# A two-layer hybrid decoder trunk on 8 cores: attention by parts of 512 keys in a ring, transposed by DMAs, with its statistics on GpSimd

## The chip, the cores and the metric

The kernel runs on 8 cores of one Trainium2 chip. Each core computes one of the 8 batch entries by itself; the cores exchange nothing. The metric is the device time in microseconds (us) of the slowest core. An execution is profiled on every core, and the profile shown is that of the slowest.

## The reference

Two layers, each with a sub-layer that mixes tokens in three parallel branches and one that mixes channels. B = 8, S = 2048, D = 1024; h @ w_in gives 7168 columns. Cut to what matters here:

```python
h = rmsnorm(x, norm_mix_pre[l]); z = h @ w_in[l]
za, zq, zk, zv, zc, zg = split(z)
ya = gmlp_branch(gelu(za), ...)                 # chunks of 128, 4 groups
yb = diff_attention(zq, zk, zv, lambda ...)     # 4 heads, q and k of 2 x 64, v of 128
yc = pool_branch(zc, w_pool, pool_scale)
merged = sum_i sigmoid(zg_i) * (y_i @ w_branch_i)
x = x + rmsnorm(merged @ w_out[l], norm_mix_post[l])
h = rmsnorm(x, norm_ffn_pre[l])
x = x + rmsnorm((silu(h @ Wg) * (h @ Wu)) @ w_ffn_out[l], norm_ffn_post[l])   # d_ff = 2816

# diff_attention, per block of 128 queries and head:
sc = q_c @ k_c.T * 64**-0.5                     # c = 0, 1; causal
w = softmax(sc_0) - lam * softmax(sc_1)
out = rmsnorm(w @ v, subln_g) * (1 - lambda_init)
```

## The kernel before, in words

Activations lie with features on the partitions. The work is cut into four stages (layer, half of the sequence): (0, 0), (0, 1), (1, 0), (1, 1), called stage 0 to 3. The feed-forward part of a stage's tokens runs in the next stage, beside that stage's attention; the last one's runs alone at the end. A stage is: projections K, V, Q; then, from stage 1 on, the feed-forward part of the stage before (`FG`, `FU` into `aT`, and `F` out of it); then the gMLP and pool branches (`gu`, `gv`, `pp` and small matmuls `mx`, `pm`, `pw`); gates of branches 0 and 2 (`G`, `B`, 16 pairs for each); gate of branch 1, which is attention's (`C` blocks); and the output projection (`O`). Behind `O` and `F` stands a norm, `tail`: sums over features by a matmul with ones (`SS`), ScalarE's `rs`, VectorE's `xn` (the residual added in `R7`), again squares and sums, and `h`, the next input in `HB`.

Attention goes by units: a unit is 128 queries and one head, 32 units in a stage. Before the change a unit's keys come in parts of up to 1024 (`key_chunks`). For each part TensorE makes both components' scores (`qk`, L1201; the diagonal's mask L1205), VectorE the row maximum (`max`, L1521), ScalarE the exponential (`exp`, L1346) into `PB`, which holds two units. Then VectorE makes the unit's factors from the sums (`w`, small operations L1422, L1551, L1425, and for two parts the rescaling L1543) and combines both components (`wk`, L1425). For every 512 keys TensorE transposes the combined weights by matmuls with the identity (`tr`, L1215), ScalarE copies the result to `WT` (`wt`), and TensorE multiplies it with V (`pv`, L1230). After four heads, ScalarE sums squares (`oc`), GpSimd makes the norm's factor (`f`), ScalarE scales (`y`), TensorE transposes (`yt`, L1241), and ScalarE writes `QY` (`ye`).

The order of each engine's work is written out beforehand by a planner, the class `Order`. It lets dense work pass one group at a time, and between groups puts in what its own clock calls ready: first `pv`, then `tr`, then the next `qk` when the progress of the dense work has reached that part's target. It has a duration for each operation, 0.2 us of lag between engines, and for a DMA its issue, its MB / 0.28, and 2.0 us. Every engine then runs its list in order and waits on semaphores. What attention has left at the fifth `C` group is run there without dense work (`finish_attention`). Weights come as blocks into four slots `WS`, cast by DMAs that GpSimd issues (`load`, L913); a block is loaded when TensorE has used the block four before. SP issues the loads of x (`x0`), of the residuals (`xo`, `xr` into `XR`, three places, each waiting for the `xn` three before), and the stores of x (`store`, 2 MB at once, when the last `xn` of a half is done).

## Time and profile before

| | |
|---|---|
| median of 3 runs | 2512.78 us (2510.51 to 2515.93) |
| profiled execution | 2516.2 us, span of its slowest core 2514.7 us |
| spans of the 8 cores | 2495.1 to 2514.7 us |
| mean granted TensorE clock, core 0 | 0.961 of 2.4 GHz |
| busy: TensorE, weight loads | 2289.6 us (91%), 1078.9 us |
| busy: VectorE, ScalarE, GpSimd | 1453.5 us (58%), 1275.8 us (51%), 289.4 us (12%) |
| mean DMA | 92 GB/s, HBM read 345 MB, written 34 MB |

Busy time is the time in which at least one instruction of the engine runs. Idle time is put down to what ended it. A group's line number is that of `kernel.py`; operations recorded by a helper have the helper's line (L1039 for dense matmuls, L1425, L1422 and L1283 for VectorE's and ScalarE's helpers), so there the tiles' names tell them apart: `ps<-HB,WS` is a matmul into PSUM from `HB` and `WS`. The timeline merges instructions of one kind that follow each other; its first two columns are the start and the length in us. The clock is the share of 2.4 GHz that the throttle granted.

### The profile page before, as it was taken

To read this page: it belongs to the slowest core of one execution; us is meant where nothing else is said; L and a number is where in the kernel's file an instruction comes from. 1 tells how busy PE (TensorE), PEld (TensorE's weight loads), DVE (VectorE), ACT (ScalarE), POOL (GpSimd) and SP (SyncE) were. 2 spreads that over 40 slices of the span, in tenths; PEclk is the share of its full clock that TensorE was granted. 3 is DMA by queue.
4 is the path that set the end of the run, shared out by engine and by line. 5 is a ranking of instruction groups with operands and counts; after the bars stand their busy time and mean duration, and the time that the engine had idled before them with its cause. 6 is when DMAs were issued, how large, how long until landed. Compare 5 with 4: busy or idle time off the path is not lost.

```text
span 2514.7 us, 39549 instructions; the slowest of 8 cores (2495.1 to 2514.7 us)
## 1 busy us (share of the span) xinstructions
PE 2289.6 (91%) x12332; PEld 1078.9 (43%) x12568; DVE 1453.5 (58%) x2618; ACT 1275.8 (51%) x2728; POOL 289.4 (12%) x573
## 2 busy tenths in 40 slices
PE   5999689999998997999998999999999899888996
PEld 2444344444443443444444444444444444333442
DVE  2467626777657884545524754567765778364313
ACT  2556635555675663634445542645667566442122
POOL 1111000000111100011011210001111111100011
PEclk9999789999998997999999999999999999889998
DMA  8433337333344442644346346643334533865458
GB/s 193 66 51 58 86 59 159 59 57 54 59 83 134 69 85 61 150 87 68 60 64 150 80 64 150 136 70 60 55 53 71 153 58 51 172 138 99 78 73 199
DMA packets 83369, 230.87 MB, mean 92 GB/s; under 512 B 8288, under 2 KB 9056, under 8 KB 82144
## 3 DMA queue, kind: packets, MB, share of 16 engines
q0 software_dynamic: 49456, 150.43, 38.0%
q1 hardware_dynamic: 33712, 77.91, 9.6%
q8 instruction: 108, 1.77, 0.3%
q14 instruction: 93, 0.76, 0.1%
HBM read 345.16 MB, written 33.55 MB: 151 GB/s over the span
## 4 chain that ended last, share of the span: by engine, by line
PE 81%; DMA 6%; DVE 5%; issue 4%; ACT 3%; POOL 0%; SPq 0%; another core or an unknown queue 0%; DVEq 0%; ACTq 0%; POOLq 0%
PE ps L1039 57%; PE ps L1080 11%; DMA WS<-wblk 4%; PE ps L1201 3%; PE ps L1130 2%; PE ps L1230 2%; PE ps L1215 2%; DVE st L1521 1%; DVE R L1425 1%; DMA R<-xT 1%; DVE R L1422 1%; PE ps L1205 1%; DVE TM L1425 1%; ACT WT L1283 1%; PE ps L1145 1%
## 5 line engine op out<-in xcount | busy, mean ns | idle before, releaser
L1039 PE MATMUL ps<-HB,WS 128*128 128x512 bf16 x4987 | 1165.7, 384 | 42.6 <-DMA WS<-wblk 19.8
L1039 PEld LDWEIGHTS ps<-HB,WS 128*128 128x128 bf16 x5120 | 493.2, 99 | 626.1 <-issue 88.7
L1283 ACT ACTIVATE TG<-ps 128x512 f32<-128x512 f32 x368 | 219.6, 597 | 526.2 <-PE ps L1039 518.7
L1521 DVE TENSOR_REDUCE st<-ps 128x1 f32<-128x1024 f32 (+7 forms) x384 | 343.2, 907 | 154.7 <-PE ps L1205 139.5
L1346 ACT ACTIVATE PB<-ps,st 128x1024 bf16<-128x1024 f32 (+7 forms) x384 | 331.2, 865 | 139.8 <-DVE st L1521 122.3
L1425 DVE SCALAR_TENSOR_TENSOR TM<-TG,ps 128x512 f32<-128x512 f32 x304 | 208.4, 686 | 321.1 <-PE ps L1039 169.9
L913 POOL DMA_DIRECT2D WS<-wblk x334 | 181.6, 544 | 1821.7 <-PE ps L1039 1472.0
L1080 PE MATMUL ps<-R,WS 128*128 128x512 bf16 x1371 | 313.2, 379 | 6.8 <-DMA WS<-wblk 2.9
L1283 ACT ACTIVATE R<-ps 128x512 f32<-128x512 f32 (+1 forms) x256 | 149.3, 596 | 230.9 <-PE ps L1080 108.9
L1039 PE MATMUL ps<-R,WS 128*128 128x512 bf16 x988 | 240.3, 381 | 6.6 <-DVE R L1422 1.9
L1425 DVE SCALAR_TENSOR_TENSOR PB<-PB,st 128x512 bf16<-128x512 bf16 (+3 forms) x320 | 204.4, 665 | 3.6
L1080 PEld LDWEIGHTS ps<-R,WS 128*128 128x128 bf16 x1408 | 133.7, 98 | 160.7 <-issue 13.4
L1039 PE MATMUL ps<-WS,HB 128*128 128x512 bf16 x747 | 184.2, 399 | 18.5 <-DMA WS<-wblk 14.2
L1283 ACT ACTIVATE WT<-ps 128x512 bf16<-128x512 f32 (+3 forms) x320 | 162.0, 532 | 72.5 <-PE ps L1215 71.4
L1283 ACT ACTIVATE HB<-R 128x512 bf16<-128x512 f32 x256 | 156.4, 628 | 38.4 <-DVE R L1422 18.2
L1039 PEld LDWEIGHTS ps<-R,WS 128*128 128x128 bf16 x1024 | 96.7, 98 | 115.0 <-issue 14.0
L1422 DVE TENSOR_TENSOR R<-TM,ps 128x512 bf16<-128x512 f32 x176 | 120.4, 684 | 40.1 <-PE ps L1039 36.6
L1230 PE MATMUL ps<-V,WT 128*128 128x128 bf16 x1088 | 110.1, 227 | 25.4 <-ACT WT L1283 23.3
L1215 PE MATMUL ps<-ident_s,PB 128*128 128x128 bf16 x1088 | 108.7, 225 | 22.4 <-DVE PB L1425 17.9
L1039 PEld LDWEIGHTS ps<-WS,HB 128*128 128x128 bf16 x768 | 75.7, 102 | 110.1 <-issue 37.4
L1230 PEld LDWEIGHTS ps<-V,WT 128*128 128x128 bf16 x1088 | 80.2, 101 | 74.8 <-issue 39.8
L1130 PE MATMUL ps<-HB,ones 128*128 128x512 bf16 x253 | 69.4, 421 | 46.9 <-ACT HB L1283 46.8
(90 smaller groups left out, 1708.9 us busy)
## 6 DMA issues: line engine op xcount, KB each, us to landing
WS<-wblk POOLq DMA_DIRECT2D x188, 512.0 KB, 5.5
WS<-wblk POOLq DMA_DIRECT2D x74, 352.0 KB, 4.6
xm<-R SPq DMA_DIRECT2D x8, 2048.0 KB, 9.5
XR<-xm SPq DMA_DIRECT2D x64, 256.0 KB, 6.3
WS<-wblk POOLq DMA_DIRECT2D x40, 384.0 KB, 5.6
R<-xT SPq DMA_DIRECT2D x16, 512.0 KB, 12.2
WS<-wblk POOLq DMA_DIRECT2D x32, 256.0 KB, 6.6
x<-R SPq DMA_DIRECT2D x4, 2048.0 KB, 10.7
```

Source lines behind the costliest of these rows:

```text
L913: e.dma_start(out=WS[:, m % NSLOT, 0:n], in_=src).then_inc(*inc(f"WS{m % NSLOT}", block, 16))
L1039: mm = e.matmul(bank(b), lh, rh, start=i == 0, stop=i == len(pairs) - 1)
L1080: mm = e.matmul(bank(C.bank[key]), w[:, k, :], aT[:, part * 11 + k, tile_of(t)], start=part == 0 and k == 0, stop=part == 1 and k == 10)
L1130: mm = e.matmul(bank(C.bank[key]), ones[:], h_buffer(kind, s)[:, c, tile_of(t)], start=c == 0, stop=c == 7)
L1201: mm = e.matmul(ps[:, 2 * comp + b, 0:m], QY[cs, h, qb * 128:(qb + 1) * 128], KT[cs, h, first + 512 * p:first + 512 * p + m], start=True, ...
L1215: mm = e.matmul(ps[:, C.bank[key], (k % 4) * 128:(k % 4 + 1) * 128], PB[:, u % 2, 0, k * 128:(k + 1) * 128], ident[:], start=True, stop=True)
L1230: mm = e.matmul(ps[:, O_BANK, h * 128:(h + 1) * 128], WT[:, rnd % 2, (k % 4) * 128:(k % 4 + 1) * 128], V[:, k, h * 128:(h + 1) * 128], sta ...
L1283: e.activation(out=out, in_=in_, func=func, scale=scale, bias=bias).then_inc(*inc(sem, key))
L1346: e.activation(out=PB[:, par, comp, first:first + n], in_=src, func=AF.Exp, bias=st[:, par, nm + comp:nm + comp + 1], scale=1.0, accum_out ...
L1422: e.tensor_tensor(out=out, in0=in0, in1=in1, op=op).then_inc(*inc(sem, key))
L1425: e.scalar_tensor_tensor(out=out, in0=in0, scalar=scalar, in1=in1, op0=op0, op1=op1).then_inc(*inc(sem, key))
L1521: e.tensor_reduce(out=col(2 if c else 0), in_=src, axis=AX.X, op=ALU.max, negate=True).then_inc(*inc("dve_max", (s, u, c, comp, "m") if c ...
```

## The change

Six things change together.

1. Keys come in parts of at most 512 (`key_chunks`). A part takes one of nine places of `PB` (`PLACES`), both components beside each other, and gives it back when its product with V is done. Its scores take two banks of PSUM, a pair in turn, instead of two or four. A unit has 1, 2, 3 or 4 parts, each with a maximum of its own; 320 parts in all (192 before), 1088 blocks of 128 keys as before.
2. The combined weights of a part are transposed by one DMA that SP issues (`tp`), from the first component's place into the second's; `tr` and `wt` are gone, and `pv` reads `PB`.
3. The unit's factors are computed on GpSimd (`wd`, `w`), in small operations in a chain; ScalarE makes one small exponential (`ee`) for units of more than one part; VectorE multiplies each part of such a unit by its factor (`p1`, 288 of them) before it combines.
4. Attention begins when Q is projected. In stage 0, V's second half, the norm of the sequence's second half, and K and V of stage 1 come after that point; in stages 2 and 3, V does. Stage 1 projects Q alone.
5. The pace of attention is set by kind of dense work (`PACE`).
6. x is stored in quarters of a half's tile (two of its eight features' blocks each) as they are ready, and a gate's `mg` waits for the end of the norm before.

The core of the diff:

```diff
+PLACES = 9
+UNITS = 4
+PACE = {"FG": 0.8, "FU": 0.8, "F": 1.35, "G": 0.7, "B": 0.7}
 def key_chunks(H, qb):
     n = (H * 8 + qb + 1) * 128
-    return [(a, min(1024, n - a)) for a in range(0, n, 1024)]
+    return [(a, min(512, n - a)) for a in range(0, n, 512)]
...
         if last:
-            w = self.op("dve", ("w", s, u), 2.0 if c else 0.8, 2, [x])
+            need = [x]
+            if c:
+                need += over
+                wd = self.op("pool", ("wd", s, u), 0.4, 1, [m])
+                need.append(self.op("act", ("ee", s, u), 0.25, 1, [wd], table=("exp", "ln")))
+            w = self.op("pool", ("w", s, u), 0.35 * c + 2.6 if c else 1.7, 1, need)
             nblk = H * 8 + qb + 1
...
+                t = self.op("sp", ("tp", s, u, r), 1.25, 0, [p], mb=0.13)
+                a["pv"].append((t, u, r, nb, r == c))
...
+        self.attention(s, total)
+        self.paused = False
+        if s != 1:
+            for ch in range(4 if s == 0 else 0, 8):
+                v(ch)
+        if s == 0:
+            self.first_norm(1, 0)
+            self.first_norm(1, 1)
+            for g in range(4):
+                for t in range(2):
+                    kq("K", g, t, 1)
+            for ch in range(8):
+                v(ch, 1)
...
+        def differences(s, u):
+            nm = stat(s, u, 0)
+            n = len(key_chunks(STAGES[s][1], u // 4))
+            g.wait_ge(*ev("dve_max", (s, u, "all")))
+            e.tensor_tensor(out=stat(s, u, 2), in0=low(s, u).unsqueeze(2).to_broadcast([128, 2, n]), in1=nm, op=ALU.subtract).then_inc(
+                *inc("pool_wd", (s, u)))
+        def weights(s, u):
+            g.wait_ge(*ev("act_exp", (s, u, n - 1, 1)))
+            if n > 1:
+                l = stat(s, u, 1)
+                g.wait_ge(*ev("act_ee", (s, u)))
+                small("pool_w", (s, u, "le"), l, l, stat(s, u, 2), ALU.mult)
...
+                small("pool_w", (s, u, "l", 1), l12, l[:, :, 0], l[:, :, 1], ALU.add)
+                for c in range(2, n):
+                    small("pool_w", (s, u, "l", c), l12, l12, l[:, :, c], ALU.add)
+            small("pool_w", (s, u, "1/l2"), c12, l12[:, 1:2], fconst[:, 4:5], ALU.pow)
+            small("pool_w", (s, u, "l1/l2"), c12, c12, l12[:, 0:1], ALU.mult)
...
+        def tp(s, u, c):
+            first, n = key_chunks(STAGES[s][1], u // 4)[c]
+            p.wait_ge(*ev("dve_w", (s, u, c)))
+            e.dma_start_transpose(out=part(s, u, c, 1).rearrange("p (k q) -> p k q", q=128), in_=part(s, u, c, 0)).then_inc(
+                *inc(f"TP{PART_AT[s, u, c] % PLACES}", (s, u, c), 16))
...
-            pe.wait_ge(*ev("act_wt", (s, u, r)))
+            pe.wait_ge(*ev(f"TP{PART_AT[s, u, r] % PLACES}", (s, u, r)))
```

Where the instructions stand now. TensorE, end of stage 0, before: the leftover of attention; `R,WS` and `QY,WS` are products of branches, `KT,QY` scores, `ident_s,PB` transposes, `V,WT` products with V, `ident_s,YB` is `yt`.

```order
L1205 MATMUL ps<-mask_s,ident_s 128x128 x2
L1230 MATMUL ps<-V,WT 128x128 x7
L1215 MATMUL ps<-ident_s,PB 128x128 x7
L1201 MATMUL ps<-KT,QY 128x512 x4
L1205 MATMUL ps<-mask_s,ident_s 128x128 x2
L1230 MATMUL ps<-V,WT 128x128 x7
L1215 MATMUL ps<-ident_s,PB 128x128 x8
L1201 MATMUL ps<-KT,QY 128x512 x4
L1205 MATMUL ps<-mask_s,ident_s 128x128 x2
L1241 MATMUL ps<-ident_s,YB 128x128 x4
L1230 MATMUL ps<-V,WT 128x128 x8
L1215 MATMUL ps<-ident_s,PB 128x128 x8
```

The same engine at the end of attention in stage 0, after:

```order
L1322 MATMUL ps<-V,PB 128x128 x16
L1146 MATMUL ps<-R,WS 128x512 x4
L1146 MATMUL ps<-HB,WS 128x512 x8
L1146 MATMUL ps<-R,WS 128x512 x4
L1146 MATMUL ps<-HB,WS 128x512 x8
L1322 MATMUL ps<-V,PB 128x128 x8
L1146 MATMUL ps<-R,WS 128x512 x4
L1322 MATMUL ps<-V,PB 128x128 x8
L1146 MATMUL ps<-HB,WS 128x512 x8
L1146 MATMUL ps<-R,WS 128x512 x4
L1146 MATMUL ps<-HB,WS 128x512 x8
L1146 MATMUL ps<-R,WS 128x512 x4
```

The transposes are gone, the products with V (now `V,PB`) stand between gates, and no row of attention is left when the gates of attention's own branch (`QY,WS`) begin.

TensorE from the end of stage 0's output projection (`R,WS` x48) to stage 1's first scores, before:

```order
L1039 MATMUL ps<-R,WS 128x512 x48
L1039 MATMUL ps<-HB,WS 128x512 x24
L1130 MATMUL ps<-HB,ones 128x512 x8
L1039 MATMUL ps<-HB,WS 128x512 x8
L1130 MATMUL ps<-HB,ones 128x512 x8
L1039 MATMUL ps<-HB,WS 128x512 x32
L1039 MATMUL ps<-WS,HB 128x512 x24
L1130 MATMUL ps<-HB,ones 128x512 x8
L1039 MATMUL ps<-WS,HB 128x512 x40
L1039 MATMUL ps<-HB,WS 128x512 x64
L1201 MATMUL ps<-KT,QY 128x512 x4
```

and after:

```order
L1146 MATMUL ps<-R,WS 128x512 x48
L1146 MATMUL ps<-HB,WS 128x512 x24
L1237 MATMUL ps<-HB,ones 128x512 x8
L1146 MATMUL ps<-HB,WS 128x512 x8
L1237 MATMUL ps<-HB,ones 128x512 x8
L1146 MATMUL ps<-HB,WS 128x512 x32
L1237 MATMUL ps<-HB,ones 128x512 x8
L1146 MATMUL ps<-HB,WS 128x512 x16
L1304 MATMUL ps<-KT,QY 128x512 x4
```

K (`HB,WS` x24 and on) and V (`WS,HB`) are gone from here; Q's eight groups are left ahead of the feed-forward part.

SP in stage 1, after (before, the 16 loads of `XR` stood in runs of 9, 2 and 5, with one load of constants and a store between them):

```order
L1102 DMA_TRANSPOSE PB<-PB 128x4x128 x3
L1102 DMA_TRANSPOSE PB<-PB 128x2x128
L1078 DMA XR<-xm 128x512 x3
L1102 DMA_TRANSPOSE PB<-PB 128x4x128 x3
L1078 DMA XR<-xm 128x512 x2
L1108 DMA x<-R 128x2x512
L1078 DMA XR<-xm 128x512
L1102 DMA_TRANSPOSE PB<-PB 128x2x128
L1078 DMA XR<-xm 128x512
```

The transposes now share the queue with the loads of `XR` and the stores of x.

## Rows read from the trace of the kernel before

**Rows 1.** The page: the span, and the engines' busy time, share and instructions.

```profile
span 2514.7 us, 39549 instructions; the slowest of 8 cores (2495.1 to 2514.7 us)
...
PE 2289.6 (91%) x12332; PEld 1078.9 (43%) x12568; DVE 1453.5 (58%) x2618; ACT 1275.8 (51%) x2728; POOL 289.4 (12%) x573
```

**Rows 2.** Waits of TensorE: who for whom, us, times, longest us.

```profile
PE ps L1039 <- DMA WS<-wblk: 34.8, 10, 8.8
PE ps L1230 <- ACT WT L1283: 23.3, 51, 1.2
PE ps L1215 <- DVE PB L1425: 17.9, 8, 4.4
```

**Rows 3.** The page's groups: the transposes, and the copies of their results.

```profile
L1283 ACT ACTIVATE WT<-ps 128x512 bf16<-128x512 f32 (+3 forms) x320 | 162.0, 532 | 72.5 <-PE ps L1215 71.4
...
L1215 PE MATMUL ps<-ident_s,PB 128*128 128x128 bf16 x1088 | 108.7, 225 | 22.4 <-DVE PB L1425 17.9
```

**Rows 4.** Timeline of TensorE, 2123 to 2131: start, us, what.

```profile
2123.21 0.39 PE L1215 MATMUL ps<-ident_s,PB 128*128 128x128 bf16 x4
2123.53 0.61 PE L1201 MATMUL ps<-KT,QY 64*128 64x512 bf16 x4
...
2129.92 0.61 PE L1215 MATMUL ps<-ident_s,PB 128*128 128x128 bf16 x8
2130.46 0.60 PE L1201 MATMUL ps<-KT,QY 64*128 64x512 bf16 x4
```

**Rows 5.** Timeline of TensorE, 282 to 328.

```profile
282.55 0.33 PE L1230 MATMUL ps<-V,WT 128*128 128x128 bf16 x3
...
324.18 0.58 PE L1241 MATMUL ps<-ident_s,YB 128*128 128x128 bf16 x4 [5.32 <-ACT YB L1283]
324.99 3.19 PE L1039 MATMUL ps<-HB,WS 128*128 128x512 bf16 x7 [0.22 <-issue]
```

**Rows 6.** Busy time in one stretch: PE, PEld, DVE, ACT, POOL, clock, DMA share, GB/s.

```profile
271.50:330.50 59.00, 31.36 (x189) 16.66 (x189) 27.82 (x45) 29.59 (x70) 4.41 (x11) 0.62 0.15 47
```

**Rows 7.** Timeline of TensorE, 949 to 976.

```profile
949.31 1.80 PE L1039 MATMUL ps<-QY,WS 128*128 128x512 bf16 x4
954.83 1.24 PE L1215 MATMUL ps<-ident_s,PB 128*128 128x128 bf16 x8 [3.71 <-DVE PB L1425]
...
975.14 0.58 PE L1241 MATMUL ps<-ident_s,YB 128*128 128x128 bf16 x4 [5.35 <-ACT YB L1283]
```

**Rows 8.** Timeline of TensorE, 2161.

```profile
2160.97 0.58 PE L1241 MATMUL ps<-ident_s,YB 128*128 128x128 bf16 x4 [5.38 <-ACT YB L1283]
```

**Rows 9.** Timeline of TensorE and VectorE, 389 to 437.

```profile
389.07 6.17 PE L1039 MATMUL ps<-HB,WS 128*128 128x512 bf16 x23
...
422.70 13.98 PE L1039 MATMUL ps<-HB,WS 128*128 128x512 bf16 x63
415.68 5.36 DVE L1425 SCALAR_TENSOR_TENSOR HB<-R,cols_s,ps 128x512 bf16<-128x512 f32 x8 [0.28 <-ACT ps L1283]
```

**Rows 10.** DMA issues on the page, and the landing of XR's alone.

```profile
WS<-wblk POOLq DMA_DIRECT2D x188, 512.0 KB, 5.5
...
XR<-xm SPq DMA_DIRECT2D x64, 256.0 KB, 6.3
...
DMA to landing us min/median/max: 2.6/6.9/24.7
```

**Rows 11.** Groups of GpSimd: a power and a product.

```profile
L949 POOL TENSOR_TENSOR gst<-gst,fconst 128x1 f32<-128x1 f32 x32 | 25.2, 787 | 4.7
L932 POOL TENSOR_TENSOR ff<-rr 128x4 f32<-128x4 f32 x32 | 7.4, 230 | 195.1 <-ACT YB L1370 183.4 <-DVE rr L1551 7.9 <-DVE PB L1425 3.2
```

**Rows 12.** The page's DMA queues: packets, MB, share of sixteen engines.

```profile
q0 software_dynamic: 49456, 150.43, 38.0%
q1 hardware_dynamic: 33712, 77.91, 9.6%
```

More of the change, by code:

```diff
@@ L425, in attention_step @@
             self.pv()
-            return True
-        if a["tr"] and len(a["pv"]) < 2 and self.there([a["tr"][0][0]], True):
-            self.tr()
             return True
@@ L483, in pv_needs @@
     def pv_needs(self):
-        need, u, r, nb, last, rnd = self.att["pv"][0]
-        return [need] + ([("y", self.att["s"], u // 4 - 1)] if u % 4 == 0 and r == 0 and u else [])
+        s = self.att["s"]
+        need, u, r, nb, last = self.att["pv"][0]
+        values = [("ev", ("V", s - 1 if STAGES[s][1] and k < 8 else s, k % 8)) for k in range(4 * r, 4 * r + nb)]
+        return [need] + values + ([("y", s, u // 4 - 1)] if u % 4 == 0 and r == 0 and u else [])
     def pv(self):
@@ L533, in qkv @@
                 kq("K", g, 1)
[L534 to L536 removed]
+        elif s > 1:
             for g in range(4):
@@ L539, in qkv @@
                     kq("K", g, t)
-            for ch in range(8):
-                v(ch)
         for g in range(4):
@@ new lines, in exp @@
+            if was:
+                a.wait_ge(*ev("pe_pv", was))
+            if len(key_chunks(STAGES[s][1], u // 4)) > 1:
+                total = stat(s, u, 1)[:, comp, c:c + 1]
+            else:
+                total = sums_of(s, u)[:, comp:comp + 1]
+                if sums_before(s, u):
+                    a.wait_ge(*ev("pool_f", sums_before(s, u)))
+            e.activation(out=part(s, u, c, comp), in_=ps[:, 2 * plan.by[s, u, c] + comp, 0:n], func=AF.Exp,
+                         bias=stat(s, u, 0)[:, comp, c:c + 1], scale=1.0, accum_out=total).then_inc(*inc("act_exp", (s, u, c, comp)))
@@ new lines, in row_max @@
+            was = unit_before(s, u)
+            if was:
+                d.wait_ge(*ev("dve_w", was + (len(key_chunks(STAGES[was[0]][1], was[1] // 4)) - 1,)))
+            e.tensor_reduce(out=stat(s, u, 0)[:, :, c], in_=ps[:, b:b + 2, 0:n], axis=AX.X, op=ALU.max, negate=True).then_inc(
+                *inc("dve_max", (s, u, c)))
+            if c and c == len(key_chunks(STAGES[s][1], u // 4)) - 1:
+                d.wait_ge(*ev("dve_max", (s, u, c)))
+                e.tensor_reduce(out=low(s, u), in_=stat(s, u, 0), axis=AX.X, op=ALU.min).then_inc(*inc("dve_max", (s, u, "all")))
@@ L1647, in dve_program @@
                 done = 1
-            if name == "w" and done == 1:
+            if name == "wk" and done == 1:
                 neg_lambda()
```

351 lines of the change are left out of this document (161 added, 190 removed).

## The prediction, made before the changed kernel ran

> **What bounds the kernel now.** I began with the page's busy shares: TensorE is busy 2289.6 of 2514.7 us, VectorE 58%, ScalarE 51%, GpSimd 12% [rows 1]. TensorE bounds, and the others matter only where it waits for them or where they hand it work late. Then I read who it waited for: weights 34.8 us, the copies of transposed weights (WT) 23.3 us, the weights that VectorE combines (PB) 17.9 us [rows 2]. These named waits are small beside the span, so the question is what TensorE itself does that could go, and where its few long waits lie. The 1088 transposing matmuls of L1215 keep it busy 108.7 us, and their 320 copies cost ScalarE 162.0 us [rows 3]. Last I read the timeline where PE's busy share falls, at the ends of the stages: there attention is left over, and is run unit after unit with nothing between, each step waiting for another engine [rows 5, 7, 8]; the clock granted in the first such stretch is 0.62 on the mean, so most of it ran at 1.2 GHz, after the engine had sat idle again and again [rows 6].
>
> **The change part by part.**
>
> (a) *Transposes leave TensorE.* In a steady stretch a group of 4 starts at 2123.21 and the next group at 2123.53, which is 0.32 us; a group of 8 takes from 2129.92 to 2130.46, 0.54 us [rows 4]. So 4 more cost 0.22 us (0.055 each) and a switch 0.10 us. 1088 x 0.055 = 60 us, and 320 groups, of which some 70 stand directly behind another of their kind, give about 250 switches x 0.10 = 25 us. That is 85 us; the bounds are 60 (no switch saved) and 109 (all that the page calls busy [rows 3]). I take 85, since the two measured starts contain the switch.
>
> (b) *The waits around them.* Of the 23.3 us for WT, some 3 lie in the leftover stretches, 20 us elsewhere; they go, as no copy is left. The waits of L1215 for PB lie nearly all in the leftovers (3.71 us in one place [rows 7]) and are not counted here.
>
> (c) *First leftover stretch* (end of stage 0). From the last product with V at 282.88 to the dense work at 324.99 there are 42.1 us [rows 5]. The order lists in it 53 transposes, 53 products with V, 5 score groups and 8 small yt matmuls. The change's order has none of this stretch: attention has begun at the queries, and its units stand between projections and gates. The work itself stays: 53 x 0.055 + 8 switches = 3.7, 5 score groups at 0.66 = 3.3, yt 0.6, together 7.6 us at full clock; the transposes are in (a) already (53 x 0.078 = 4.1). 42.1 - 7.6 - 4.1 = 30 us. The 7 dense matmuls behind it took 3.19 us where 7 take 1.5 at full clock, so 2 us more. Gain 32; bounds 20 (the same units then stall the dense work among which they stand) and 36.
>
> (d) *Second leftover* (end of stage 1), 951.1 to 975.1: 24.0 us, in which 32 products with V, one score group and one yt remain (3.6 us) and 32 transposes are counted (2.5). 18 us, and 1 for the slow clock behind it [rows 7]. Gain 19, bounds 10 and 20.
>
> (e) *Third* (stage 3): the wait of 5.38 us before a yt [rows 8], plus about 2 us of slow clock behind it. Gain 7. Stage 2 has no leftover.
>
> (f) *Cover taken away at the start of stage 1.* Before, the last output projection ends at about 389 and 24 projection groups (K, V, Q, 41 us) run while VectorE makes h; h of the first half is ready at 415.4, of the second at 421.0 [rows 9]. The change has already projected this stage's K and V, so only Q is left: 8 x 1.73 + 4 sums x 1.73 = 20.7 us, until 409.8 (a group of 8 matmuls takes 1.73 us at 0.22 each, as in the 63 from 422.70 on). TensorE then waits 5.6 us, does 3.5 us of the first half, waits 2.1 us more: 8 us idle, and 3 for the clock behind it (the 7 matmuls above after a like gap). Loss 11; bounds 6 and 18. Stages 2 and 3 keep K and Q ahead and V behind: nothing there.
>
> (g) *More score groups.* Parts of 512 instead of 1024 keys make 320 groups of 192: 128 more switches x 0.10 = 13 us lost. In return a score group waits for two banks of PSUM, not four.
>
> (h) *New waits.* Product with V now waits for a DMA. The planner's costs give it 1.25 us to issue, 0.13 MB / 0.28 = 0.46 us to move, 2.0 to land and 0.2 of lag: 3.9 us behind VectorE, and put the product into the order right there. No transposing DMA is in the trace. The nearest rows are SP's loads of 256 KB into XR: they land in 2.6 us at least and 6.9 at the median [rows 10]. At the low end nothing waits, at the high end each of the 128 units is 3.0 us late: 0 to 384 us. The low end is nearer: these DMAs move half the bytes, touch no HBM, and come singly, while XR's come three at a time beside weight loads. With (i) I take 0.3 us for each of 128 units, 38 us.
>
> (i) *The queues that they pass.* On SP 320 transposes now stand in one order with the XR loads, each of which waits for VectorE's xn three places before, at least 1.5 us. A transpose behind such a load waits for it, and the product with V in TensorE's order waits with it. This is confined to the ends of the feed-forward parts in stages 1 to 3; at 5 to 10 us each it is the larger part of the 38 us. On GpSimd there are 864 small operations: at 0.23 us and about 0.15 between, with 128 powers at 0.79 [rows 11], about 395 us; with the 289 of before 27% of the span. The 334 weight loads stand behind them. What hides this: four slots of weights, so that a load is issued three blocks ahead (a feed-forward block is 32 matmuls, 6.9 us, and more with attention between them), and lands in 5.5 us [rows 10]. Priced at zero; without that cover each unit's statistics (3 to 4 us) would hold a load back, at most 128 x 3.5 = 450 us. VectorE loses its scalar chain and gains 288 multiplications of 512; ScalarE loses 162 us of copies and gains 256 exponentials with their fixed part. Neither comes nearer to the span.
>
> (j) *x in quarters*: SP issues 4 stores for 1 as each pair of tiles is ready. The bytes are the same, and TensorE's waits name no store: zero.
>
> Sum: -85 - 20 - 32 - 19 - 7 + 11 + 13 + 38 = -101 us. From the profiled execution's 2516.2 us this gives 2415 us; the median of the runs, 2512.8, is 3 us below that execution, well inside what I can resolve.
>
> One rule speaks against (a). The row says that a block costs TensorE 85/1088 = 0.078 us. The Trainium skill (VectorE: DVE Perf Modes, "The three transpose paths") prices a 128x128 block at 390 ns on TensorE and 1309 ns by DMA, and advises TensorE wherever PSUM will do as the destination. By its figure the 1088 blocks would be an estimated 1424 us of DMA time, 57% of the span if each block held all sixteen engines, and the DMA would be the bound.
>
> **Rivals.**
>
> 1. *Forecast, chance 0.57*: 2365 to 2475, with (h)+(i) between 0 and 0.8 us a unit.
>
> 2. *Most of it is given back, 0.20*: products with V come 0.8 to 1.1 us late per unit: TensorE waits 100 to 140 us, 2477 to 2511. For it: one DMA in the chain instead of a copy of 0.6 us, and an order fixed beforehand, in which a late landing stops TensorE at once. Against it: the order before was fixed too, and its WT waits were 51 of at most 1.2 us [rows 2].
>
> 3. *Slower, 0.12*: the DMA engines hold it up. Place: the queue shared by weight loads (38.0% of sixteen engines) and SP's (9.6% for 33712 packets, 0.115 us each) [rows 12]. A transpose of 4 blocks is 512 runs of 256 bytes; at a packet's price for each run, 139264 runs x 0.115 / 16 = 1000 us, 40% more; by bytes (35.7 MB, where 77.9 MB took 9.6%) only 4.4% more. At 40% the engines are at 88% and landings go to 6.9 us and beyond: 3 us late for 128 units, 2516 - 139 + 384 = about 2760. It decides from 1.1 us a unit on (139 / 128), where the gains before (h) are used up. A spread from 2518 to 2760. The skill's figure above would come out here, or higher.
>
> 4. *More than forecast, 0.08*: nothing waits, leftovers vanish wholly, score groups cost no switch: 2325 to 2365.
>
> 5. *The change does nothing that can be measured, 0.03*: rival 2 at its edge. 0.2% is 5 us, about what a measurement of this kernel tells from no change.
>
> **How the numbers follow.** The time is that of case 1: 2415 us. Its own range holds 0.57; adding rival 2 up to about 2503 brings it to 0.75, and the upper edge of rival 4 from 2355 on to 0.8. Range 2355 to 2503. Faster: 0.57 + 0.20 + 0.08 = 0.85; same 0.03; slower 0.12.
>
> **What would show it.** PE busy falls by about 100 us (a, g). No stretch with only attention on TensorE, and a mean granted clock over 0.97 (c, d, e). A wait of 5 to 8 us for HB after Q in stage 1 (f). Products with V wait for the DMA PB<-PB: about 20 to 60 us in total if I am right, over 140 if rival 3 is; its median landing under 3.9 us behind VectorE in the first case, over 5 in the other, and then the DMA share near 85%. GpSimd near 27% busy with no rise of TensorE's 34.8 us for weights (i); a rise to over 80 would make GpSimd's order the error. The prediction fails if the transposes' landing is far from 2 to 4 us, or if the units moved among gates stall them as often as they stalled alone.

## Result, and the profile after

The changed kernel takes 2495.65 us (median), before 2512.78 us (five executions of each): ratio 0.9926, 95% interval 0.9908 to 0.9944, so 17 to 19 us faster. A second measurement (e5 below) gives 0.9904 (0.9888 to 0.9921), 24 us. Ratios leave out executions in which one die ran at a lower clock, so they are not always the quotient of the medians. The forecast was 101 us faster; a fifth to a quarter of it came. The sign and the outer range held, the size did not.

The page of the changed kernel, beside [rows 1] and [rows 12]:

```profile
span 2493.6 us, 39436 instructions; the slowest of 8 cores (2460.3 to 2493.6 us)
...
PE 2257.4 (91%) x11480; PEld 1011.1 (41%) x11480; DVE 1451.9 (58%) x2304; ACT 1205.4 (48%) x2905; POOL 540.6 (22%) x1437
...
q0 software_dynamic: 49456, 150.43, 38.5%
q1 hardware_dynamic: 183792, 113.60, 19.6%
```

TensorE's busy time reads 32 us lower, but the page of before lacks 236 matmuls (12332 beside 12568 weight loads). Other cores of the same executions have them all; core 1 before, then after:

```profile
PE 2296.7 (92%) x12568; PEld 1076.1 (43%) x12568; DVE 1453.8 (58%) x2618; ACT 1275.7 (51%) x2728; POOL 289.4 (12%) x573
```

```profile
PE 2250.7 (91%) x11480; PEld 1011.3 (41%) x11480; DVE 1452.3 (58%) x2304; ACT 1205.4 (49%) x2905; POOL 536.9 (22%) x1437
```

Six cores of each execution are complete in this way. On their mean TensorE was busy 2294.9 us before and 2250.2 after: 45 us less, where 100 were forecast. Its idle time, the rest of the span, went from 207.4 to 225.4 us. The transposes added 150,080 packets and 35.7 MB to SP's queue for 10.0% more of the sixteen engines (19.6 against 9.6), near the low end of rival 3's two bounds (4.4% and 40%). Each transposing DMA, from its own line:

```profile
L1102 SPq DMA_TRANSPOSE PB<-PB x320: 1095/1192/5436, 85.5 to 2099.6; - x160
...
DMA to landing us min/median/max: 2.2/3.9/15.7
```

It holds SP 1.19 us at the median and lands 3.9 us after its issue at the median; the planner had 1.25 + 0.46 + 2.0 = 3.7. Counted from the end of VectorE's combination, the median is 4.1 us (planner: 3.9), and a quarter of the 320 take over 6.0. Waits of TensorE (who for whom, us, times, longest), beside [rows 2]:

```profile
PE ps L1237 <- ACT HB L1375: 68.3, 9, 17.0
PE ps L1322 <- DMA PB<-PB: 41.9, 25, 7.2
PE ps L1146 <- DMA WS<-wblk: 39.8, 14, 7.7
PE ps L1146 <- DVE HB L1504: 13.3, 3, 8.4
```

The wait for the DMA is 41.9 us, where 38 were forecast; weights went from 34.8 to 39.8 only. But the first line, the sums of squares waiting for ScalarE's squares, is 68.3 us, where the same line before (L1130) had 46.8, and only the 3.8 us of it in stage 1 are named by the prediction (f). Its longest, 17.0, is the start of the program, which before had too (18.0). What is new is the second in length, 16.68 us in stage 0, where attention has just begun. TensorE's timeline there (start, us, what, idle before):

```profile
90.65 0.40 PE L1307 MATMUL ps<-mask_s,ident_s 128*128 128x128 bf16 x2
107.72 3.19 PE L1237 MATMUL ps<-HB,ones 128*128 128x512 bf16 x8 [16.68 <-ACT HB L1375]
112.33 0.22 PE L1322 MATMUL ps<-V,PB 128*128 128x128 bf16 x1 [1.41 <-DMA PB<-PB]
115.70 3.57 PE L1237 MATMUL ps<-HB,ones 128*128 128x512 bf16 x8 [3.16 <-ACT HB L1375]
...
126.43 1.31 PE L1146 MATMUL ps<-HB,WS 128*128 128x512 bf16 x5 [3.66 <-DVE HB L1504]
```

The releaser named is ScalarE, which squares x; follow it one step on. It waits itself, for the loads of x:

```profile
94.60 1.15 ACT L1375 ACTIVATE HB<-R 128x512 bf16<-128x512 f32 x2 [3.97 <-DMA R<-xT]
...
103.33 1.15 ACT L1375 ACTIVATE HB<-R 128x512 bf16<-128x512 f32 x2 [5.64 <-DMA R<-xT]
```

SP's queue at the same time:

```profile
85.50 1.19 SPq L1102 DMA_TRANSPOSE PB<-PB  x1
86.79 11.38 SPq L1069 DMA_DIRECT2D R<-xT  x8
98.27 42.32 SPq L1102 DMA_TRANSPOSE PB<-PB  x9
```

The eight loads of x for the second half of the sequence stand behind the first transposing DMA, which waits for VectorE's combined weights of the first unit; they hold SP 11.38 us, land 7.7 to 19.6 us after their issue, and the second transposing DMA stands behind them. Before, the same eight loads began at 28.56 us. TensorE has nothing to do meanwhile, and its clock goes down (PE, PEld, DVE, ACT, POOL busy, clock, DMA share, GB/s):

```profile
60.00:90.00 30.00, 24.87 (x121) 10.70 (x121) 9.95 (x31) 7.91 (x28) 5.98 (x15) 0.94 0.42 70
90.00:120.00 30.00, 8.44 (x24) 2.92 (x25) 7.79 (x13) 12.45 (x29) 3.48 (x12) 0.56 0.78 183
```

A granted clock of 0.56 over 30 us is mostly 1.2 GHz; the 8 matmuls at 107.72 take 3.19 us where 8 take 1.73 at 2.4 GHz.

At the start of stage 1 the waits are those of term (f), 3.79 + 1.24 + 3.51 = 8.5 us of idleness against 8 forecast:

```profile
434.96 3.41 PE L1237 MATMUL ps<-HB,ones 128*128 128x512 bf16 x8 [3.79 <-ACT HB L1375]
439.61 3.61 PE L1146 MATMUL ps<-HB,WS 128*128 128x512 bf16 x16 [1.24 <-DVE HB L1504]
446.74 0.62 PE L1304 MATMUL ps<-KT,QY 64*128 64x512 bf16 x4 [3.51 <-DVE HB L1504]
```

Two stage marks make kernels comparable. They are read from TensorE's timeline on core 0: the first and last mixing matmul (ps<-wsT_s,VN) and the first and last matmul on the attention's output (ps<-QY,WS) of a stage. Lengths in us, e-kernels as described below:

```
                                        before  after(e5)   e6     e13    e15    e14    e16    e17
start to first mixing, stage 0          111.3   185.2     104.2  171.8  103.8  161.2  105.6  162.3
first to last QY,WS, stage 0             95.1    48.6      75.9   50.5   84.9   51.1   85.5   51.6
from there to first mixing, stage 1     414.8   379.6     429.0  411.1  400.9  390.5  393.1  374.5
first to last QY,WS, stage 1             77.1    47.9      49.2   50.0   48.6   48.4   50.4   48.3
end of stage 1's to end of stage 3's   1207.0  1198.9    1232.0 1226.4 1193.8 1194.0 1178.1 1167.4
```

Before to after: the leftovers did go (95.1 to 48.6, 77.1 to 47.9, 76 us together, of which some 18 was work: units that moved, and transposes that are gone). But the start of stage 0 became 73.9 us longer. Of this 27.7 are the 16 moved groups of K and V (16 x 1.73), which come off the third line, and some 8 are units placed there (my estimate from their matmuls). The rest, near 38 us, is new. On the mean of the six complete cores TensorE's idle time in these stretches changed like this: last gates of stage 0 from 26.6 to 6.0 us, of stage 1 from 19.5 to 7.3, start of stage 0 from 34.5 to 61.2, and all the rest from 126.8 to 150.9.

### The profile page after: what moved, and what is told of

The parts are those of the page before. It is cut to its first block, busy times and chain, and to the rows that moved or that the text cites. A ratio compares the mean times of both kernels' runs of the same rounds, so it can differ in the third digit from the quotient of the medians.

```text
span 2493.6 us, 39436 instructions; the slowest of 8 cores (2460.3 to 2493.6 us)
## 1 busy us (share of the span) xinstructions
PE 2257.4 (91%) x11480; PEld 1011.1 (41%) x11480; DVE 1451.9 (58%) x2304; ACT 1205.4 (48%) x2905; POOL 540.6 (22%) x1437
## 3 DMA queue, kind: packets, MB, share of 16 engines
q1 hardware_dynamic: 183792, 113.60, 19.6%
## 4 chain that ended last, share of the span: by engine, by line
PE 73%; DMA 14%; DVE 6%; issue 3%; ACT 2%; SPq 1%; POOL 0%; DVEq 0%; ACTq 0%; POOLq 0%
PE ps L1146 53%; PE ps L1187 10%; DMA PB<-PB 7%; DMA WS<-wblk 4%; PE ps L1304 3%; PE ps L1322 2%; PE ps L1237 2%; DMA R<-xT 2%; DVE R L1504 1%; DVE R L1501 1%; DMA XR<-xm 1%; PE ps L1307 1%; DVE HB L1504 1%; ACT L1375 1%; PE ps L1252 1%
## 5 line engine op out<-in xcount | busy, mean ns | idle before, releaser
L1146 PE MATMUL ps<-HB,WS 128*128 128x512 bf16 x5120 | 1193.7, 385 | 57.3 <-DMA WS<-wblk 36.9
L1440 ACT ACTIVATE PB<-ps,st 128x512 bf16<-128x512 f32 (+3 forms) x640 | 393.8, 621 | 219.7 <-DVE st L1605 205.0
L978 POOL DMA_DIRECT2D WS<-wblk x334 | 187.9, 563 | 1249.1 <-PE ps L1146 975.9
L1605 DVE TENSOR_REDUCE st<-ps 128x2 f32<-128x1024 f32 (+3 forms) x320 | 338.8, 1062 | 194.3 <-PE ps L1304 133.8
L1187 PE MATMUL ps<-R,WS 128*128 128x512 bf16 x1408 | 323.8, 383 | 4.7 <-DMA WS<-wblk 4.5
L1146 PE MATMUL ps<-R,WS 128*128 128x512 bf16 x1024 | 246.8, 383 | 4.3 <-DVE R L1501 4.1
L1504 DVE SCALAR_TENSOR_TENSOR PB<-PB,st 128x512 bf16<-128x512 bf16 (+3 forms) x320 | 214.7, 671 | 60.9 <-POOL st L991 29.0
L1375 ACT ACTIVATE HB<-R 128x512 bf16<-128x512 f32 x256 | 155.5, 626 | 57.9 <-DMA R<-xT 27.9
L1146 PEld LDWEIGHTS ps<-R,WS 128*128 128x128 bf16 x1024 | 96.9, 98 | 118.3 <-issue 15.7
L1322 PE MATMUL ps<-V,PB 128*128 128x128 bf16 x1088 | 101.1, 220 | 42.6 <-DMA PB<-PB 41.9
L1237 PE MATMUL ps<-HB,ones 128*128 128x512 bf16 x256 | 72.0, 432 | 68.3 <-ACT HB L1375 68.3
L1440 ACT ACTIVATION_READ_ACCUMULATOR PB<-ps,st 128x1 f32 x640 | 129.1, 202 | 0.0
L1304 PE MATMUL ps<-KT,QY 64*128 64x512 bf16 (+3 forms) x640 | 114.0, 357 | 10.4 <-ACT PB L1440 6.9
L1322 PEld LDWEIGHTS ps<-V,PB 128*128 128x128 bf16 x1088 | 75.3, 98 | 94.5 <-issue 60.7
```

Of the source, the lines that this page charges most:

```text
L978: e.dma_start(out=WS[:, m % NSLOT, 0:n], in_=src).then_inc(*inc(f"WS{m % NSLOT}", block, 16))
L1146: mm = e.matmul(bank(b), lh, rh, start=i == 0, stop=i == len(pairs) - 1)
L1187: mm = e.matmul(bank(C.bank[key]), w[:, k, :], aT[:, part * 11 + k, tile_of(t)], start=part == 0 and k == 0, stop=part == 1 and k == 10)
L1237: mm = e.matmul(bank(C.bank[key]), ones[:], h_buffer(kind, s)[:, c, tile_of(t)], start=c == 0, stop=c == 7)
L1304: mm = e.matmul(ps[:, b + comp, 0:n], QY[cs, h, qb * 128:(qb + 1) * 128], KT[cs, h, first:first + n], start=True, stop=not diag)
L1322: mm = e.matmul(ps[:, O_BANK, h * 128:(h + 1) * 128], w[:, (k - 4 * r) * 128:(k - 4 * r + 1) * 128], V[:, k, h * 128:(h + 1) * 128], start ...
```

## The experiments

Each was measured in 5 rounds beside the kernel before. Chips differ in how wide the intervals come out, so kernels are compared within a row where possible. 1% is 25 us.

### First row: what does each moved piece cost?

**e1**: in `qkv`, the second half's norm goes ahead of attention.

```diff
+        if s == 0:
+            self.first_norm(1, 0)
+            self.first_norm(1, 1)
         self.attention(s, total)
...
         if s == 0:
-            self.first_norm(1, 0)
-            self.first_norm(1, 1)
```

> One part of the change taken back: the norm of the second half of the sequence (with its 8 loads of x) is planned again ahead of attention's start in stage 0, and not behind attention's first parts and V. Theory A (the loads stand on SP behind the first transposing DMA, so h comes late and TensorE waits 27 us between 90 and 126 us, at half clock around it): the waits of 16.7 and 3.7 us go, the stretch up to stage 0's first mixing matmul gets 25 to 40 us shorter, and the time is 2455 to 2470 us. Rival B (GpSimd's first statistics or the first units themselves would hold TensorE there anyway): the same stretch stays, 2488 to 2500 us.

**e2**: no transposing DMA is issued, so the products with V take weights that were not transposed.

```diff
-            pe.wait_ge(*ev(f"TP{PART_AT[s, u, r] % PLACES}", (s, u, r)))
-            w = part(s, u, r, 1)
+            pe.wait_ge(*ev("dve_w", (s, u, r)))
+            w = part(s, u, r, 0)
```

> Leaves the transposition out: no transposing DMA is issued, the products with V take the weights untransposed, as soon as VectorE has combined them; the planned order is that of the changed kernel. It bounds from above what the DMA transposes cost. Theory A (they cost what TensorE's waits for them name, 41.9 us, a part of which other waits take over): 2450 to 2475 us. Rival B (150,080 more packets and SP's queue slow the weight loads and the XR loads as well): 2360 to 2430 us, with the waits for WS and XR falling too. Rival C (the first waits only move to the next releaser): 2485 to 2498 us.

**e3**: the order of before within a stage. K and V of stage 1 are in stage 1, and attention begins behind all projections; so that GpSimd doesn't wait for a lambda that stands behind its own work, VectorE computes lambda ahead of its first `vn`.

```diff
-        elif s > 1:
+            for ch in range(4, 8):
+                v(ch)
+        else:
             for g in range(4):
                 for t in range(2):
                     kq("K", g, t)
+            for ch in range(8):
+                v(ch)
         for g in range(4):
             for t in range(2):
                 kq("Q", g, t)
+        if s == 0:
+            self.first_norm(1, 0)
+            self.first_norm(1, 1)
         self.attention(s, total)
...
```

What the changed kernel had behind `self.attention` is gone from there, and the planner's total of dense work (`projections`) is set to fit, as it is in e7, e10 and e11.

> Attention is begun after all projections of its stage again, and K and V of stage 1 are projected in stage 1, as before the change; parts of 512, ring, transposing DMAs, GpSimd's statistics and quarters stay. Theory A (beginning at the queries gained 44 us at the end of stage 0 and 25 at the end of stage 1, and lost 38 at stage 0's start, 8 for units moved there and 11 at the start of stage 1): 12 us over the changed kernel, 2500 to 2515 us. Rival B (without TensorE's transposes the leftover stretches are short anyway, so an early start only loses): 2455 to 2480 us.

**e4**: GpSimd's table loads.

```diff
-            if name == "rst" and args == [1, 7]:
+            if name == "w" and args == [1, 31]:
                 tables(1)
```

> GpSimd's four loads of the second layer's tables, which wait 15.4 us at 823 us for a TensorE matmul and hold up statistics and weight loads behind them, are put behind the statistics of stage 1's last unit. Theory A (new work queued behind this old wait makes the section of mixing and gates in stage 1 20 us longer): 2480 to 2490 us, 5 to 15 us under the changed kernel. Rival B (units and weights behind it have cover enough): 2491 to 2498 us.

Measured: e1 0.9792 (0.9733 to 0.9851); e2 0.9670 (0.9609 to 0.9731); e3 0.9719 (0.9661 to 0.9777); e4 0.9849 (0.9777 to 0.9921). For e1 theory A holds. Its timelines on core 0, SP first, then TensorE:

```profile
83.85 26.16 SPq L1103 DMA_TRANSPOSE PB<-PB  x7
```

```profile
90.02 3.57 PE L1238 MATMUL ps<-HB,ones 128*128 128x512 bf16 x8 [4.40 <-ACT HB L1376]
...
96.37 0.28 PE L1305 MATMUL ps<-KT,QY 64*128 64x256 bf16 x2 [1.37 <-ACT PB L1441]
...
101.42 2.81 PE L1147 MATMUL ps<-HB,WS 128*128 128x512 bf16 x7 [2.33 <-DVE HB L1505]
```

The loads of x are gone from among the transposing DMAs, and 16.68 us of idleness became 4.40. The stretch to the first mixing is 24 us shorter than in the changed kernel's first profile (162.2 against 186.2), just under the 25 to 40 that were expected.

e1 moves the norm together with its loads. That the queue matters by itself is seen in e2, and in e13 below, which transposes on TensorE. Both leave the norm behind attention, but have no transposing DMA ahead of the loads. SP and TensorE in e2, then in e13:

```profile
28.90 16.92 SPq L1069 DMA_DIRECT2D R<-xT  x8
93.20 3.57 PE L1234 MATMUL ps<-HB,ones 128*128 128x512 bf16 x8 [4.89 <-ACT HB L1372]
```

```profile
27.79 15.51 SPq L1079 DMA_DIRECT2D R<-xT  x8
89.58 3.57 PE L1247 MATMUL ps<-HB,ones 128*128 128x512 bf16 x8 [1.80 <-ACT HB L1396]
```

The loads begin at 28 or 29 us instead of 87, and 4.89 or 1.80 us of idleness stand where 16.68 stood. Up to the first mixing TensorE is idle 49.8 us in both (mean of six complete cores), 61.2 in the changed kernel and 43.3 with the norm first (e14): the queue made 11 us of it, the norm's place the next 6 or 7.

e3 went to the rival's side: undoing the early start made the kernel faster, not slower. So the gain from it, the prediction's largest after the transposes, was a loss as a whole. e2 lies between the bounds of theories A and B: 2.3% or 59 us under e5 (below), a part of which is e1's gain, since its loads of x are early too; B's sign is absent, as its wait for weights is 41.9 us, beside 39.8 in the changed kernel. e4 removed GpSimd's wait of 15.38 us for TensorE (0.3 in its trace), which stood here:

```profile
838.40 0.62 POOL L985 DMA_DIRECT2D VN<-tri  x1 [15.38 <-PE ps L1281]
```

but its interval overlaps the changed kernel's, and e8 shows no gain from it either: not settled, and small.

### Second row: the transposes alone

**e5** is the changed kernel again.

> The changed kernel once more, as the point to which the others of this row are compared on one chip. By its first measurement: ratio to before 0.9926, some 17 us under it.

**e6**: e3 with the transposes back on TensorE.

```diff
-                t = self.op("sp", ("tp", s, u, r), 1.25, 0, [p], mb=0.13)
-                a["pv"].append((t, u, r, nb, r == c))
+                a["tr"].append((p, u, r, nb, r == c))
...
+            for k in range(min(4, nblk - 4 * r)):
+                mm = e.matmul(ps[:, C.bank[key], k * 128:(k + 1) * 128], part(s, u, r, 0)[:, k * 128:(k + 1) * 128], ident[:],
+                              start=True, stop=True)
...
+            run("act_wt", (s, u, r), part(s, u, r, 1), ps[:, C.bank["tr", s, u, r], 0:n], AF.Copy)
```

> The kernel of e3 (attention begun after all projections) with the transposes back on TensorE: groups of up to 4 against ident into a PSUM bank, copied by ScalarE into the same place of the ring to which the DMA wrote; statistics, ring and parts stay. The difference to e3 is what moving the transposes to DMAs is worth with everything else equal. Theory A (as forecast: 85 + 20 gained, 38 given back): 67 us over e3, near before's time or above it (ratio 0.995 to 1.005). Theory B (the saving is smaller, since the waits for the DMA, 50 us in e3, take back most of the 60 to 85): 10 to 40 us over e3, ratio 0.976 to 0.988. Theory C (the DMA gains nothing): ratio 0.968 to 0.975.

**e7**: e1's edit and e4's, and K and V of stage 1 in stage 1, with attention still begun at the queries.

```diff
-        elif s > 1:
+        else:
...
-            for g in range(4):
-                for t in range(2):
-                    kq("K", g, t, 1)
-            for ch in range(8):
-                v(ch, 1)
```

> Attention begins at the queries in every stage, as in the changed kernel, but the norm of the second half stands ahead of it (as in e1), K and V of stage 1 are projected in stage 1 again, and GpSimd's loads of the second layer's tables stand late (as in e4). Theory A (moving K and V into stage 0 uncovered h at the start of stage 1, 8.5 us of waits there, and spread few units over a long stretch): 8 to 20 us under e1, ratio 0.971 to 0.976. Rival B (moved cover is paid back by the room it gives to stage 0's units, whose leftover stretch then returns): as e1 or over it, 0.979 to 0.985.

**e8**: e3 and e4's edit, and in the planner

```diff
-                    self.op("sp", ("out", s, t, oc), 0.1, 1, [("xn", kind, s, t, oc, n)], mb=0.5)
+                    self.op("sp", ("out", s, t, oc), 1.3, 1, [("xn", kind, s, t, oc, n)], mb=0.5)
```

and the same for `xr`, `store` and (1.4) `x0`.

> The kernel of e3 with the planner's price of a load or store on SP at 1.3 us (1.4 for x0) in place of 0.1, and the tables late as in e4. In the trace one such issue takes 1.2 to 1.4 us on SP, so that the transposing DMAs behind several of them start later than planned, and the products with V stand too early in TensorE's order. Theory A (this is what the waits for the DMA are made of): they fall from 50 us to under 25, ratio 0.958 to 0.966. Rival B (they come from the waits inside the XR loads, or from late statistics, which a price does not change): ratio 0.969 to 0.974, waits for the DMA over 40 us.

Measured: e5 0.9904 (0.9888 to 0.9921); e6 1.0076 (1.0062 to 1.0090); e7 0.9826 (0.9807 to 0.9845); e8 0.9779 (0.9764 to 0.9794). e6 against e15 (0.9765, below, the same kernel with DMAs) is 3.1%, 78 us: theory A and a little more. The page of e6 shows what came back to TensorE and ScalarE, much as in [rows 3]:

```profile
L1392 ACT ACTIVATE PB<-ps 128x512 bf16<-128x512 f32 (+3 forms) x320 | 165.6, 534 | 84.5 <-PE ps L1323 82.6
...
L1323 PE MATMUL ps<-ident_s,PB 128*128 128x128 bf16 x1088 | 111.3, 223 | 24.3 <-DVE PB L1527 16.5
```

e7 cannot be told from e14 (0.9836, e1 again): rival B, moving K and V was neutral in the sum. e8 is no faster than e15 (0.9765): its waits for the DMA are 43.6 us still, as rival B has it, but its ratio lies above the ranges of both. Its price was also read wrongly: in the changed kernel's trace an `xr` holds SP 0.33 us at the median and a `store` 0.36 or 0.43, not 1.2 to 1.4, so 1.3 overprices them. How the right price would do was not tried.

### Third row: where does the early start lose?

**e9** is e3 again, and **e12** is e3 with e2's edit, so it transposes nothing. **e10** and **e11** are e3 with these:

```diff
-            for ch in range(4, 8):
-                v(ch)
...
         self.attention(s, total)
         self.paused = False
+        if s == 0:
+            for ch in range(4, 8):
+                v(ch)
```

```diff
             self.gmlp_pool(s)
             self.paused = False
+            if s == 0:
+                self.keys_of_stage_1()
             self.gates(s)
```

Here `keys_of_stage_1` is stage 1's 8 groups of K and 8 of V, taken out of its own `qkv`.

> The kernel of e3 once more, as the point of comparison for this row. By e3 and e8: ratio to before 0.972 to 0.980.

> As e9, but stage 0 begins its attention at the queries (norm of the second half ahead of it, K and V of stage 1 left in stage 1); stages 1 to 3 begin late. Theory A (the loss by an early start is stage 0's: its first units stall TensorE between the last projections and gu): 8 to 15 us over e9. Rival B (it is made in stages 1 to 3, where units spread over V and the mixing section meet late statistics and XR loads): within 4 us of e9.

> As e9, but the 16 projection groups of K and V of stage 1 (27.6 us) stand between the mixing section and the gates of stage 0, with attention running among them, so that they cover stage 0's last units. Theory A (stage 0's last section still takes 85 us where 48 are needed; the cover takes most of these 37, less 8 to 11 at the start of stage 1, where only Q is left beside h): 12 to 25 us under e9, ratio 0.966 to 0.973, which would be the fastest of all. Rival B (the last units are bound by chains through VectorE, ScalarE and GpSimd that take as long with cover): within 5 us of e9, or over it.

> As e9 without any transposition (products with V take the weights untransposed, as in e2), in the same planned order. It tells what the DMA transposes still cost where attention begins late. Theory A (the 44 to 50 us that TensorE waits for them, some of it passed on to other waits): 25 to 40 us under e9, ratio 0.962 to 0.968. Rival B (they also slow weight and XR loads): 50 us and more under e9.

Measured: e9 0.9734 (0.9671 to 0.9797); e10 0.9775 (0.9722 to 0.9829); e11 0.9783 (0.9713 to 0.9852); e12 0.9576 (0.9526 to 0.9625). e10 tells nothing apart: it is 10 us over e9, with an interval of that difference of 21 us either way. e11 is 0.5% over e9, 12 us, with an interval of that difference from -11 to +36 (both intervals' halves squared and summed): theory A's 12 to 25 us of gain are unlikely. e12 is 1.6% or 40 us under e9, 20 either way, which is theory A's range but does not exclude rival B's 50. B's sign is absent: TensorE's wait for weights (`ps<-HB,WS`) is 31.7 us in e12 and 30.4 in e9.

### Fourth and fifth row: the whole table, and the place of the products

**e13** is the changed kernel with e6's edit of the transposes; **e14** is e1 and **e15** is e3 again. **e16** is e3 with one number of the planner changed, the time at which it takes a transposing DMA to have landed:

```diff
-            end = self.dma_free + 2.0
+            end = self.dma_free + (3.5 if label[0] == "tp" else 2.0)
```

**e17** is e1 with the same; **e18** is e16 with 5.0 in place of 3.5.

> The changed kernel with its transposes back on TensorE (the edit of e6, here with attention begun at the queries). Theory A (the leftover stretches are made by TensorE's own transposes and their copies, so that with these the early start gains, as forecast: 20 to 47 us under e6): ratio 0.989 to 1.000. Rival B (the early start loses with either kind of transpose, since its price is the start of stage 0 and the cover of stage 1): ratio 1.012 to 1.025, 10 to 40 us over e6.

> The kernel of e1 once more, beside e15. Theory A (of the 30 us that the early start costs, the norm behind the first transposing DMA is about 20): ratio 0.981 to 0.985, and 6 to 15 us over e15. Rival B (the norm is all of it): within 4 us of e15.

> The kernel of e3 and e9, as the point of comparison of this row: ratio 0.973 to 0.979.

> As e15, but the planner takes a transposing DMA to land 1.5 us later than it did, so that a product with V stands later in TensorE's order; nothing else changes. Theory A (TensorE waits for the DMA because the order puts the product where the planner believes it landed): the waits for the DMA fall from some 45 to under 20 us, and the time by 10 to 25 us. Rival B (the landing is late by another's wait in front of it, of which the place in the order knows nothing, or the lateness is passed on to ScalarE's exponentials by the ring): the waits stay over 30 us, the time within 5 us.

> The kernel of e1 (early start, norm first) with e16's margin of 1.5 us on the planner's landing. Theory A (the margin acts on products with V wherever they stand): ratio 0.972 to 0.976, 20 to 28 us under e14, and still 12 to 25 us over e16, the rest of the early start's loss. Rival B (the rest of that loss is itself products placed too early): ratio 0.965 to 0.969, as e16.

> As e16 with a margin of 3.0 us. Theory A (16 us of waits for the DMA are left, of which a further margin takes half, while the ring of nine places makes the next exponentials later): ratio 0.961 to 0.967, within 10 us of e16. Rival B (the ring runs full, ScalarE's exponentials wait for TensorE's products and TensorE's score groups for them): over e16, 0.968 to 0.975.

Measured: e13 1.0141 (1.0117 to 1.0164); e14 0.9836 (0.9817 to 0.9856); e15 0.9765 (0.9738 to 0.9792); e16 0.9659 (0.9640 to 0.9678); e17 0.9655 (0.9593 to 0.9717). e13 fell on rival B's side, so the early start loses with either kind of transpose. e14 is 18 us over e15, a little more than theory A's 15. e16 is theory A, with slightly more gain than expected. e18 has no ratio; in its profiled execution cores 0 to 3 have a median span of 2418.4 us, e16's 2416.6, so a further margin brought nothing that can be seen, though the waits for the DMA went down again, from 16.4 to 9.0 us.

In a table, ratio to before:

```
                          transposes on TensorE   by DMA          by DMA, landing priced 1.5 us later
early, norm behind        1.0141 (e13)            0.9904 (e5)     -
early, norm first         -                       0.9836 (e14)    0.9655 (e17)
late                      1.0076 (e6)             0.9765 (e15)    0.9659 (e16)
```

Waits of TensorE in e15, then in e16:

```profile
PE ps L1318 <- DMA PB<-PB: 39.6, 34, 3.5
PE ps L1142 <- DMA WS<-wblk: 32.9, 13, 7.5
```

```profile
PE ps L1318 <- DMA PB<-PB: 16.4, 19, 2.4
PE ps L1142 <- DMA WS<-wblk: 22.5, 10, 7.1
```

and in e14, then in e17:

```profile
PE ps L1323 <- DMA PB<-PB: 38.6, 31, 3.1
```

```profile
PE ps L1323 <- DMA PB<-PB: 9.2, 7, 3.4
```

The order of work is fixed when the kernel is built. With the planner's landing near the median of the real one, a product with V stands where a late DMA stops TensorE at once. 1.5 us of margin put it later in the order. That took 23 us of waits and 27 us of time from the late kernel (1.06%), and 29 us of waits and 45 us of time from the early one (1.8%, interval some 16 us either way). e16 and e17 are the fastest that compute the whole reference: 3.4% under the kernel before and 2.5% to 2.7% under the changed one. With the margin, the early start loses nothing against the late one that can be seen (e17 against e16, 1 us less, 16 either way): e17's rival B held.

## Why the prediction was wrong

**Transposes, waits for copies, new waits: (a), (b), (h), (i), right.** Forecast -85 - 20 + 38 = -67 us. Measured by themselves: 78 us with the late start (e6 to e15), 60 with the early one (e13 to e5). On the complete cores TensorE's busy time falls by 73 us in both pairs (2315.3 to 2242.3, 2323.0 to 2250.2). The parts of it fit too: without any transposition e12 is 5.0% under e6, 125 us, where (a) and (b) say 105; the price of the DMAs is e12 to e15, 1.9% or 47 us (14 either way), where (h) and (i) say 38.

**DMA load, rival 3, excluded.** 10.0% of sixteen engines for 150,080 packets is 0.10 x 2493.6 x 16 / 150,080 = 0.027 us a packet, a quarter of the 0.115 of SP's packets before. For a block of 128x128 all sixteen together are taken 249/1088 = 0.23 us. The figure of the Trainium skill (VectorE: DVE Perf Modes, "The three transpose paths"), 1309 ns a block, does not hold as occupation here, and its advice in favour of TensorE (same page, "Rules for kernel authors") would have cost 60 to 78 us.

**The steps that failed: (c) to (e), which took a stretch gone as time gained, with (i) and the size of (g).** The prediction took "the change's order has none of this stretch" as a gain of 32, 19 and 7 us for (c), (d), (e), and charged the early start 11 us (f). The stretches did shrink, and the idleness of (f) is as forecast. But of TensorE's idle time the 33 us that left the two stretches came back as 27 at the start of stage 0 and 24 elsewhere. What failed is threefold:

1. *A queue that was not followed.* (i) names the XR loads and the weight loads as what the transposing DMAs stand among. The change's description says that the second half's norm comes behind `attention`, but no term follows its eight loads of x, which then stand behind a DMA that waits for the first unit's whole chain. Putting the norm first gave 24 us in that stretch and 0.7% of the time (0.9904 to 0.9836), 17 us.

2. *A gain put down to the wrong cause.* Stage 1's leftover stretch goes from 77.1 to 49.2 us in e6 and 48.6 in e15, which both begin late, e6 with TensorE's transposes. So (d) belongs to what e6 keeps of the change (which part was not tried), not to beginning at the queries. The wait of (e) is gone in e6 and e15 too. In stage 0 it is otherwise: e6 has 75.9 of 95.1 left, e15 84.9, and only the early start brings it to 51.1 (e14). But it lengthens other stretches by more than that, and as a whole it cost 0.65% (16 us, e6 to e13) with TensorE's transposes and 1.4% (35 us, e15 to e5) with DMAs: e3 fell on the rival's side of the expectation.

3. *(g) was too cheap.* e6 has parts, ring, GpSimd's statistics, `PACE` and the quarters of x, but neither DMA transposes nor the early start. It is 0.76% slower than before, 19 us, though its two leftover stretches are 47 us shorter (19.2 and 27.9). The other stretches of core 0 together are some 50 us longer; up to 18 of these are units that moved. On the complete cores TensorE is busy 2315.3 us for 2294.9, 20 more, and idle 198.5 for 207.4. The scores account for the 20: the same 640 matmuls, of the same mean, in 320 groups for 192. Before, then e6:

```profile
L1201 PE MATMUL ps<-KT,QY 64*128 64x512 bf16 (+3 forms) x640 | 94.3, 357 | 3.5 <-ACT PB L1346 3.5
```

```profile
L1310 PE MATMUL ps<-KT,QY 64*128 64x512 bf16 (+3 forms) x640 | 113.9, 356 | 0.8 <-ACT PB L1457 0.6
```

That is 19.6 us for 128 more groups, 0.15 each, where (g) has 0.10 and 13 us. Why idleness fell by only 9 us, with 18 less in the two stretches, no run separates: e6's trace has 640 exponentials of 512 (395.6 us on ScalarE) for 384 wider ones (331.2), and each unit has a chain of small steps on GpSimd. This stays open.

**The sum again, with what was measured:** +19 for all of the change but DMAs and early start (e6), -78 for the DMAs (e15), +35 for the early start (e5): -24 us, against -101. In (c) to (g) the forecast has -34 where the runs have +54; the rest was 11 us better than forecast.

**The early start's loss:** of its 35 us, 17 were the norm. The other 18 cannot be seen any more when products with V are priced to land later (e17 against e16). That speaks for products placed too early, but does not settle it: with TensorE's transposes, where no DMA has to land, the early start lost 16 us as well (e6 to e13), and no margin was tried there. The waits for the DMA that the margin removed, 29 us, are not all of the 45 gained (e14 to e17): on the complete cores idle time fell by 36 us and busy time by 14; from e15 to e16 by 17 and 9. Why the busy time falls is not shown.

**Signs given beforehand.** The DMA wait of 20 to 60 us: right. A landing under 3.9 us behind VectorE: 4.1, just missed, far from rival 3's 5. The weights' wait under 80: right, though 34.8 rose to 39.8. GpSimd 22% for 27 forecast. PE busy down by 100: wrong, 45; the terms named for it, (a) and (g), give 72 by the prediction's own sum, not 100, and measured are 73 less and 20 more, with 8 more from the early start (e15 to the changed kernel). A mean clock over 0.97: wrong, 0.959 to 0.965 on the eight cores. Rival 2 gave the right size (2477 to 2511) but for another reason: its products with V did not wait the 100 to 140 us that it asks for.

**x in quarters (j)** and the ring's nine places were not tried by themselves.

## What to carry to other kernels

When work is moved, print the whole order of every queue at the new place and ask of each entry what it now stands behind: here putting eight loads and their norm back ahead of one waiting DMA gained 17 us, as much again as the whole change. Measure the pieces of a compound change as a table (early or late, TensorE or DMA) before crediting any of them. Where an order is fixed beforehand, price a landing above its median: here 1.5 us more gained 27 and 45 us, and a further 1.5 brought nothing that can be seen. And count busy time only on cores whose matmul records are complete.

## What the runs showed of the hardware

A transposing DMA of 128x512 bf16 from SBUF to SBUF holds SP's queue 1.19 us, lands in 3.9 us at the median (2.2 to 15.7), and takes sixteen engines 0.78 us (249/320). That it slows the large weight loads is not settled: they land in 5.9 us with it and without it under the early start (e2), in 6.2 and 5.5 under the late one (e15, e12). Its packets, 238 bytes on the mean (35.7 MB / 150,080), took a quarter of the time of SP's packets before, which carried 2.3 KB. The same 640 score matmuls kept TensorE busy 94.3 us in 192 groups and 113.9 in 320. And idleness is dearer than it reads: after 16.68 us of it the next 8 matmuls took 3.19 us for 1.73, and the 30 us around it were granted a clock of 0.56.
